# Norm weights folded into rope tables and transposed copies in two attention groups of a two-block kernel

## The reference

```python
for l in range(2):
    x = x + 0.5 * swiglu(rms_norm(x, ffn1_norm[l]), ...)          # D_FF = 2816
    h = rms_norm(x, mix_norm[l])
    pa, pb, pc, pd = jnp.split(h @ w_in[l], IN_SPLITS, axis=-1)
    ya = neighbourhood_mixer(pa, ...)      # group A (1): 4 heads of 64
    yb = mla_mixer(pb, ...)                # group B (2): 4 heads of 96 = 64 nope + 32 rope
    yc = diff_mixer(pc, ...)               # group C (3): differential attention
    yd = gqa_mixer(pd, ...)                # group D (4): 4 query heads, 2 key heads of 64
    x = x + jnp.concatenate([ya, yb, yc, yd], axis=-1) @ w_out[l]
    x = x + 0.5 * swiglu(rms_norm(x, ffn2_norm[l]), ...)
    x = rms_norm(x, final_norm[l])

# group B: q and k of 96; the rope turns the last 32
q, k = rms_norm(q, q_norm), rms_norm(k, k_norm)                   # weight per channel
q = concat([q[..., :64], apply_rope(q[..., 64:], ang)]); k = ...  # the same
y = softmax(q @ k.T * 96**-0.5) @ v
# group D: q has 4 heads, k and v have 2; the rope turns all 64, as two axes of 32
q, k = rms_norm(q, q_norm), rms_norm(k, k_norm)
q, k = axial_rope(q, ang_row, ang_col), axial_rope(k, ang_row, ang_col)
y = softmax(q @ k.T * 64**-0.5) @ v        # query heads 0, 1 use key head 0; 2, 3 use key head 1

def apply_rope(x, ang):                    # halves x1, x2
    return concat([x1 * cos - x2 * sin, x1 * sin + x2 * cos])
```

## Time and profile before

| | us |
|---|---|
| median of three runs (lowest, highest) | 1319.37 (1311.88, 1321.9) |
| the profiled execution, its own time | 1319.89 |
| its span, first to last instruction | 1317.6 |
| TensorE (PE) busy in the span | 1265.6 (96%) |
| VectorE (DVE) busy | 841.5 (64%) |
| ScalarE (ACT) busy | 640.0 (49%) |
| GpSimd (POOL) busy | 78.7 (6%) |
| mean granted TensorE clock | 0.968 |

### The profile page before, as it was taken

One profiled execution on the slowest core, in us unless ns is written; L12 is line 12 of the kernel. 1 busy time (PEld: TensorE's weight loads), 2 busy tenths in 40 slices (PEclk: granted clock), 3 DMA queues, 4 the chain that ended last, 5 costly groups with the idle time before them and its releaser, 6 DMA issues.

```text
span 1317.6 us, 24755 instructions
## 1 busy us (share of the span) xinstructions
PE 1265.6 (96%) x10500; PEld 1239.5 (94%) x10500; DVE 841.5 (64%) x1059; ACT 640.0 (49%) x850; POOL 78.7 (6%) x57
## 2 busy tenths in 40 slices
PE   6999999988999999999999997999999999999997
PEld 6999999978999999999999996899999989899995
DVE  5766677775676666876667686476666754446665
ACT  4433346754543334533335764453333554766542
POOL 1110011210000000000000211000000000000000
PEclk9999999986999999999999995799999999999999
DMA  8876665320565655566665530256655655415542
GB/s 287 219 227 206 191 224 172 114 87 2 182 200 193 191 191 192 170 199 195 194 219 163 166 132 12 65 165 219 192 191 191 200 178 174 128 58 168 176 152 105
DMA packets 169514, 220.33 MB, mean 167 GB/s; under 512 B 5280, under 2 KB 152480, under 8 KB 169312
## 3 DMA queue, kind: packets, MB, share of 16 engines
q1 hardware_dynamic: 165680, 213.66, 50.8%
q0 software_dynamic: 2080, 2.48, 1.0%
q10 hardware_dynamic: 1680, 3.13, 0.7%
HBM read 218.15 MB, written 3.42 MB: 168 GB/s over the span
## 4 chain that ended last, share of the span: by engine, by line
PE 86%; ACT 6%; DVE 5%; issue 1%; DMA 1%; SPq 0%; POOLq 0%; POOL 0%; DVEq 0%; ACTq 0%
PE pj L433 12%; PE pj L437 12%; PE pj L436 12%; PE acc L437 8%; PE acc L436 8%; PE acc L433 8%; PE tr L433 6%; PE tr L437 6%; PE tr L436 6%; PE acc L616 4%; ACT probs L994 2%; ACT w_hi L875 1%; PE tr L608 1%; DVE w_lo L1186 1%; PE tr L586 1%
## 5 line engine op out<-in xcount | busy, mean ns | idle before, releaser
L1186 DVE TENSOR_TENSOR w_lo<-raw,w_hi 128x2048 fp32r<-128x2048 f32 (+2 forms) x206 | 459.4, 2230 | 241.7 <-ACT w_hi L875 240.3
L875 ACT ACTIVATE w_hi<-raw 128x2048 fp32r<-128x2048 f32 (+2 forms) x206 | 381.2, 1854 | 395.3 <-PE pj L433 142.0
L433 PE MATMUL pj<-hT_hi,w_hi 128*128 128x256 f32 x992 | 277.2, 279 | 3.0 <-DVE w_lo L1186 2.4
L437 PE MATMUL pj<-hT_hi,w_lo 128*128 128x256 f32 x992 | 275.8, 278 | 0.0
L436 PE MATMUL pj<-hT_lo,w_hi 128*128 128x256 f32 x992 | 275.7, 278 | 0.0
L437 PE MATMUL acc<-act_hi,w_lo 128*128 128x256 f32 x704 | 194.3, 276 | 0.0
L433 PE MATMUL acc<-act_hi,w_hi 128*128 128x256 f32 x704 | 194.3, 276 | 0.0
L436 PE MATMUL acc<-act_lo,w_hi 128*128 128x256 f32 x704 | 194.3, 276 | 0.0
L433 PEld LDWEIGHTS pj<-hT_hi,w_hi 128*128 128x128 f32 x992 | 187.5, 189 | 4.5 <-DVE w_lo L1186 2.6
L436 PEld LDWEIGHTS pj<-hT_lo,w_hi 128*128 128x128 f32 x992 | 187.3, 189 | 0.0
L437 PEld LDWEIGHTS pj<-hT_hi,w_lo 128*128 128x128 f32 x992 | 187.1, 189 | 0.0
(11 more groups left out here) (212 smaller groups left out, 1989.6 us busy)
## 6 DMA issues: line engine op xcount, KB each, us to landing
raw<-in_w_in SPq DMA_DIRECT2D x47, 1024.0 KB, 5.3
raw<-in_ffn_w_up SPq DMA_DIRECT2D x44, 1024.0 KB, 5.3
raw<-in_ffn_w_down SPq DMA_DIRECT2D x44, 1024.0 KB, 5.0
raw<-in_ffn_w_gate SPq DMA_DIRECT2D x43, 1024.0 KB, 5.4
raw<-in_w_out SPq DMA_DIRECT2D x12, 1024.0 KB, 4.9
raw<-in_w_proj_a SPq DMA_DIRECT2D x4, 512.0 KB, 3.5
raw<-in_w_proj_b SPq DMA_DIRECT2D x4, 512.0 KB, 3.9
raw<-in_w_proj_c SPq DMA_DIRECT2D x4, 512.0 KB, 3.4
```

The lines of the kernel that those rows point to most:

```text
L433: ins = pe.matmul(out, lhs[0], rhs[0], start=first, stop=False, **kw)
L437: return pe.matmul(out, lhs[1], rhs[0], start=False, stop=last, **kw)
L875: act.activation(w_hi[r % RING][:, 0:w], raw[r % RING][:, 0:w], ACT.Copy).then_inc(hi_set, 1)
L1186: dve.tensor_tensor(w_lo[r % RING][:, 0:w], raw[r % RING][:, 0:w], w_hi[r % RING][:, 0:w].bitcast(F32), ALU.subtract).then_inc(lo_set, 1)
```

## The change

Arithmetic per output stays the same up to rounding; the work is placed differently.

- B: the norm weights of the 64 channels that aren't turned, and the softmax scale in those of q and k, are applied as a scale per partition in ScalarE's copy of the transposes (column `K_B` of `cols`, q's and k's). For the 32 turned channels the weights are in the rope tables, and `K_B` holds the softmax scale or 1.
- D: weights in the rope tables; the scale 0.125 as an immediate in ScalarE's copy of the transposed queries.
- A new function, `rope_tables`, makes both tables once per layer on VectorE, between the two halves of the computation of `lam`. D's table lies in `diag`.
- `rotate` handles both token tiles in one instruction where the access pattern allows it; for D, queries and keys are turned in two calls.
- D's keys aren't written twice. ScalarE's evacuation of the query block (`D0`) puts the heads in the order 0, 2, 1, 3, so that a query head lies on the partitions of its key head; `turn D` transposes six blocks instead of eight.
- The `tensor_scalar` on the row maxima of B and D goes; the exponential has scale 1.
- The walk through `ORDER` is written as `ORDER_ACT` and `ORDER_DVE`, with the calls of `look_ahead` as steps of their own; the sequence on each engine stays.

```diff
-K_FFN1, ..., K_FINAL, NCOL = 0, 8, 16, 24, 32, 34, 35, 37, 39, 47
+K_FFN1, ..., K_FINAL, K_B, NCOL = 0, 8, 16, 24, 32, 34, 35, 37, 39, 47, 49
+        mla_rope = sb("mla_rope", [P, 2, T * 2 * 32])
+        gqa_rope = diag[:].rearrange("p a b -> p (a b)").rearrange("p (i n) -> p i n", i=2)
-        turned = pooledT[:, 2:4, :].rearrange("p a b -> p (a b)")
+        turned = pooledT[:].rearrange("p a b -> p (a b)")
...
-                            turn_blocks(f0, pair_blocks(proj, D0, 2) + doubled(), P)
+                            turn_blocks(f0, pair_blocks(proj, D0, 3), P)
...
-            def copy_fills(f0, n, dst, rows=P, gain=None, l=0):
+            def copy_fills(f0, n, dst, rows=P, gain=None, l=0, per=1):
-                    by = {} if gain is None else {"scale": col(l, gain + m)}
+                    by = {} if gain is None else {"scale": col(l, gain + m // per)[0:rows]}
...
+            def copy_gqa(f0):
+                for m in range(2):
+                    wait_tr_full(act, f0 + m)
+                    by = {} if m else {"scale": 0.125}
+                    act.activation(qkT[QKT["D"]][:, 2 * m:2 + m, :].rearrange("p a b -> p (a b)"),
+                                   tr[(f0 + m) % 2][:, 0:4 - 2 * m, :].rearrange("p a b -> p (a b)"),
                                    ACT.Copy, **by).then_inc(tr_free[(f0 + m) % 2], 1)
...
-            def rotate(v, heads, base, width, axes, ctab, stab, signal):
-                for t in range(T):
...
+            def rotate(v, tables, axes, signal):
+                _, n, heads, width = v.shape
+                b = turned[:, 0:n * heads * width].rearrange("p (n h d) -> p n h d", n=n, h=heads)
+                cv, sv = [x.unsqueeze(2).to_broadcast((P, n, heads, width)) for x in tables]
+                if axes == 1:
                     for hf in range(2):
...
+                        step_(dve.tensor_tensor(b[:, :, :, d], v[:, :, :, e], sv[:, :, :, d], ALU.mult))
+                else:
+                    for hf in range(2):
+                        for t in range(n):
+                            ins = dve.tensor_tensor(halves(b, axes, hf)[:, t], halves(v, axes, 1 - hf)[:, t],
+                                                    halves(sv, axes, hf)[:, t], ALU.mult)
+                        step_(ins)
+                step_(dve.tensor_tensor(v, v, cv, ALU.mult))
+                step_(dve.tensor_tensor(v, v, b, ALU.add), signal)
+
+            def rope_tables(l):
+                dve.wait_ge(tables_in, 16)
+                for dst, at, n, w, axes, ctab, stab in ((mla_rope, R_MLA, 96, 32, 1, I_MC, I_MS),
+                                                        (gqa_rope, R_GQA, 64, 64, 2, I_GC, I_GS)):
+                    gain = row[:, at:at + 2 * n].rearrange("p (q n) -> p q n", q=2)[:, :, n - w:n]
+                    for t in range(T):
...
+                        dve.tensor_tensor(cd, cos, gain, ALU.mult)
+                        for hf in range(2):
...
+                            ins = dve.tensor_tensor(pick(sd, hf), pick(sin, hf), pick(gain, 1 - hf), ALU.mult)
+                step_(ins)
...
                 step_(dve.tensor_reduce(lam[:, 0:2], sl, AX_X, ALU.add), lam_in)
+                rope_tables(l)
                 dve.wait_ge(lam_exp, l + 1)
...
-                            v = normalize(l, k, vec)
-                            gains(v, R_MLA, (4, 4), 96, vec)
-                            rotate(v, 8, 64, 32, 1, I_MC, I_MS, prep_set)
+                            normalize(l, k, vec)
+                            rotate(qk_b.rearrange(...)[:, :, :, 64:96], [...], 1, prep_set)
...
-                            gains(v, R_GQA, (4, 2), 64, vec)
-                            rotate(v, 6, 0, 64, 2, I_GC, I_GS, vec)
-                            copy_twice(D0 + 256, prep_set)
+                            rotate(v[:, :, 0:4, :], [x[:, :, 0, :] for x in ropes], 2, vec)
+                            rotate(v[:, :, 4:6, :], [x[:, :, 1, :] for x in ropes], 2, prep_set)
...
-                                step_(dve.tensor_reduce(mx, ps, AX_X, ALU.max, negate=True))
-                                step_(dve.tensor_scalar(mx, mx, 96 ** -0.5 if m == "B" else 0.125, None, ALU.mult), max_set)
+                                step_(dve.tensor_reduce(mx, ps, AX_X, ALU.max, negate=True), max_set)
```

## The result

The change makes the kernel slower: 1348.08 us, the median of four runs (1345.35 to 1351.71), beside 1320.63 for the kernel before (four runs, 1311.88 to 1326.71). The ratio is 1.023, 95% interval 1.018 to 1.029: 27 us lost where I had forecast 0.3 gained. The profiled execution has a span of 1343.1 us, 25.5 more than before.

A forecast was written before the change was run, and what follows sets the result against it. TensorE, busy 96% of the span, was taken as the bound, so only its waits could gain. Per layer -0.42 + 0.26 = -0.16 us, twice -0.3, took 1319.89 to 1319.6; counted from the median, 1319.1 us, range 1310 to 1322.5.

The forecast's parts named there:

- the sum: All terms together: per layer -0.42 + 0.26 = -0.16 us, twice -0.3; bounds -0.8 and +0.7.
- something that I hadn't seen: Only an unseen cause would pass the 1% threshold: faster 5%, slower 3%.
- Tables: Twelve VectorE instructions of `rope_tables` ahead of `take_over`: 1.8 us, costing TensorE 0, at most 0.2 per layer.
- prep B: VectorE's preparation of B: 4.1 us instead of 6.9, gaining nothing because TensorE is still at projections.
- prep D: VectorE's preparation of D: about 5.3 us against 6.75, gaining nothing, covered by TensorE's `pv 5` and scores.
- from `turn B`'s copy to the exponentials: B's copies on the path cost 0.26 us more per layer; the first `tensor_scalar` removed saves 0.21.
- from the start of unit 7's output to that of unit 8's exponentials: Second place where a removed `tensor_scalar` was on the path: unit 8's exponentials about 0.2 us earlier.
- the wait behind `turn D`: TensorE's wait for ScalarE's first copy stays at 3.3 us; fewer transposes and a shorter second copy gain zero.
- The clock rival: TensorE's granted clock changes its step in the attention stretch: 1312.2 us, or 1320.8 if it falls earlier; 12%.
- VectorE on the path: Hidden waits for both preps would make their relief count: 8.6 us less, 1310.5 us; 4%.
- The tables' delay: Tables of 3.5 us delay `take_over`, making TensorE 1.0 us late at the last `hT_lo` per layer: 1321.1; 12%.
- the copies' scale: B's copies cost 0.26 us twice and the removed instructions don't pay, ScalarE pacing the exponentials: 1319.9 us; 4%.

The follow-up runs named there:

- e13: The changed kernel with 224 unused bytes right behind `cols`, every address as in the kernel before modulo 256: 1313.38 us, ratio 0.996.
- e9: The changed kernel with 224 unused bytes before `raw`: 1336.42 us, ratio 1.018.
- e16: The kernel before with 32 unused bytes before `diag` and 224 before `raw`: 1318.35 us, ratio 1.000.

## Why the prediction was wrong

**The step that failed** is a term that the sum put at nothing: every matmul outside the edits was left at its old duration, and the new column of `cols` and the new table `mla_rope` were costed by their instructions and not by their bytes. I read the earlier trace rows, TensorE busy for 96%, as "only its waits can change". Its pace could: where `w` lies against `hT` and `act`, and where `ones` lies, moved by 32 bytes each, and the FFNs went from 113.3 ns to 117.4 and 118.7. That term is 28.0 us of the profiled 25.5 more; the forecast for everything else was 0. I gave 3% to a loss by something that I hadn't seen.

**The edited steps** went as predicted. Tables 1.7 us (1.8 forecast), without a wait behind them; `prep B` 4.1 (4.1), `prep D` 5.2 (5.3), both hidden; from `turn B`'s copy to the exponentials +0.07 (+0.05); from the start of unit 7's output to that of unit 8's exponentials 3.52 us instead of 3.73 (0.2 less forecast); the wait behind `turn D` 3.5 us at the longest (3.3). With its addresses restored the changed kernel is at 0.996 of the kernel before (0.993 to 0.999), and with `hn` moved besides at 0.997 (0.993 to 1.001), where the sum said 0.9998. The first interval lies just below it and the second holds it. Whether the edits are worth more than 0.3 us or the scatter, of the clock and of the states of entry, made that difference stays open: the mixers of `e13` took 161.4 and 160.8 us, of the profile before 161.3 and 162.8.

**The clock rival** named the scatter: mixers of 154.8 to 164.3 us in kernels with the same work. It isn't the result; in this profile it hid up to 6.5 of the 28.0 us. **VectorE on the path** promised 8.6 us less. The mixers of `e13`, with the shorter preps, are 1.9 us shorter in sum than those of the profile before, and none of TensorE's longer waits names a prep; the times alone don't refute it, since an interval from 0.993 has room for 8.6 us. **The tables' delay** and **the copies' scale** are refuted by the rows above.

That the pace hangs on d, and that d = 0 is the worst, points to the reads of a product's two operands getting in each other's way; no row shows the stall itself, so this is argued and not shown. The Trainium skill (SBUF — State Buffer, the section "A bandwidth-pool intuition that's wrong") gives weight loads a second independent read port beside that of the moving operand. By that, d should make no difference; the runs with nothing but unused bytes added say that it does, 113.3 ns against 120.0. The same page's part on operand start alignment speaks of which addresses are legal and says that its runs timed nothing; here 32 bytes within what is legal cost 2.5%.

The Trainium skill (TensorE: Matmul & The Clock Gate, the section "Wait — 56ns, not 53.3ns?") gives N / 2.4 GHz and about 2.5 ns between the starts of warm matmuls, an estimated 109.2 ns for 256 columns. The best pace that any kernel here shows is 113.3, 4 ns above that, and the worst 120.0.

## What to carry to other kernels

Where TensorE is full, a new tensor or one more column is an edit of the hot loop: compare the number of matmuls in a window of a stretch that the change doesn't touch before looking at the edits. If that number moved at the same granted clock, put the old addresses back with unused bytes and time the change again; here that turned a ratio of 1.023 into 0.996, the lowest of the case. Judge a change and its placement in two experiments, not in one, and by several runs of each: one trace shows which pace a stretch got in that execution, and another may get the other.

## What the runs showed of the hardware

- **The pace of back-to-back fp32 matmuls of 256 columns depends on where their two operands start relative to each other modulo 256 bytes**: between starts 120.0 ns at d = 0, 118.3 at 32, 113.3 or 117.8 at 64, 117.4 or 118.7 at 96, 118.7 at 128, 117.8 at 192, 116.7 at 224, over 1,495 matmuls each; FFNs at the same pace agree to about 0.1 us. With the roles of the two exchanged, 192 and 224 give what 64 and 32 gave, mostly. d = 160 wasn't tried, nor were other widths.
- **At d = 64, and at 96, there are two paces, and a stretch nearly always keeps the one that it begins with**, in `e9` 117.8 ns for 180 us, until a short matmul breaks it. From where that matmul loads has a part in it: FFNs at 113.3 ns in 20 of 20 with `ones` at 32, in 1 of 12 at 64. It isn't all: the same stretch of `e16` went at 117.8 ns in one layer and 113.3 in the other.
- **The duration of one matmul hardly tells it**: the timeline gives 0.28 us at either pace, the means by group are 276 and 280 ns. Starts and counts do.
